# Six stages of a half share one block with named waits, and the last gate projection moves behind the attention

## What is computed

```python
h = _rmsnorm(x, norm_mix_w)
z, xbc, dt_raw, q, kv_c, kv_s, kv_w, nsa_g, br_g = _split_proj(h @ w_in)
y_ssm = mamba(z, xbc, dt_raw)                          # 32 heads, state 128
o = g0 * compressed_attention + g1 * selected_attention + g2 * window_attention
mix = sigmoid(br_g[0]) * (y_ssm @ w_ssm_branch) + sigmoid(br_g[1]) * (o @ w_attn_branch)
x = x + mix @ w_out
x = x + peer(_rmsnorm(x))     # per token 8 heads x 16 experts out of 16384, rows of peer_u, then of peer_v
y = _rmsnorm(x)
```

## Time and profile before

| | |
|---|---|
| median of 3 runs | 2726.63 us (2724.88 to 2726.69) |
| profiled execution, its time | 2727.99 us |
| its span in the trace | 2726.0 us |
| PE, DVE, POOL busy, share of the span | 74%, 54%, 54% |
| mean granted TensorE clock | 0.865 of full speed |

### The profile page before, as it was taken

How to read it: one execution, slowest core, us unless ns; L and a number is a source line. 1 busy time by engine, 2 the same in 40 slices (tenths; PEclk the granted TensorE clock), 3 DMA queues, 4 the chain that set the end, 5 groups by cost and what they waited for, 6 DMA issues and landing times. The chain is left out here.

```text
span 2726.0 us, 31394 instructions
## 1 busy us (share of the span) xinstructions
PE 2013.4 (74%) x10926; PEld 1272.5 (47%) x10926; DVE 1463.7 (54%) x3522; ACT 663.9 (24%) x1977; POOL 1472.5 (54%) x1487
## 2 busy tenths in 40 slices
PE   8999989988877989989989935754177776554054
PEld 6778865666655657644454622332154442111010
DVE  4421023247999965557621769778776764016800
ACT  5441026224545210025611122310021110000000
POOL 1110000016566865647644777777767777557775
PEclk9999989989987999989989967767589997877577
DMA  5424454446886999979889889999999999999998
GB/s 182 169 78 140 141 182 158 163 151 226 293 325 201 400 377 369 374 285 371 317 348 397 291 286 391 412 392 326 382 353 411 411 410 394 403 386 409 352 406 311
DMA packets 209781, 843.32 MB, mean 309 GB/s; under 512 B 25753, under 2 KB 32729, under 8 KB 190105
## 3 DMA queue, kind: packets, MB, share of 16 engines
q0 software_dynamic: 170912, 644.95, 62.3%
q1 hardware_dynamic: 38712, 196.36, 19.3%
HBM read 821.80 MB, written 23.54 MB: 310 GB/s over the span
## 5 line engine op out<-in xcount | busy, mean ns | idle before, releaser
L3658 POOL DMA_INDIRECT e_ring<-in_peer_u,e_idx x523 | 613.2, 1173 | 301.9 <-DVE e_dot L3822 139.0
L3822 DVE CUSTOM_DVE_ANT_0 e_ring<-e_ring,e_h 128x1024 f32<-128x1024 f32 x523 | 632.7, 1245 | 73.0 <-DMA e_ring<-in_peer_u,e_idx 25.8
L3658 POOL DMA_INDIRECT e_ring<-in_peer_v,e_idxT x487 | 506.0, 1039 | 261.6 <-issue 133.7
L3725 PE MATMUL ps<-e_ring,e_wz 128*32 128x512 f32 x1948 | 323.2, 712 | 269.4 <-DMA e_ring<-in_peer_v,e_idxT 147.4
L3725 PEld LDWEIGHTS ps<-e_ring,e_wz 128*32 128x32 f32 x1948 | 67.3, 121 | 427.3 <-issue 423.4
L371 PE MATMUL ps<-hT_ahead,wb 128*128 128x320 f32 x384 | 114.4, 454 | 0.0
L371 PEld LDWEIGHTS ps<-hT_ahead,wb 128*128 128x128 f32 x384 | 75.4, 201 | 31.2 <-issue 6.0
L3866 DVE TENSOR_TENSOR e_x<-e_x,ps 128x512 f32<-128x512 f32 x10 | 6.4, 683 | 145.7 <-PE ps L3725 145.7
L3725 PE MATMUL ps<-ring_pair,e_wz 128*32 128x512 f32 x152 | 69.7, 797 | 17.9 <-DMA e_ring<-in_peer_v,e_idxT 11.3
L1861 POOL CAST ra_atf<-ra_at 128x32 f32<-128x32 uint32 x8 | 1.7, 212 | 149.7 <-DVE ra_hit L1854 149.7
L1229 POOL MEMSET inda<- 128x256 f32 x1 | 0.3, 312 | 147.7 <-POOLq L4133 147.7
(11 more groups left out here) (789 smaller groups left out, 4577.3 us busy)
## 6 DMA issues: line engine op xcount, KB each, us to landing
wb<-in_weights SPq DMA_DIRECT2D x65, 1024.0 KB, 7.8
e_ring<-in_weights SPq DMA_DIRECT2D x36, 1024.0 KB, 4.9
wb<-in_late_weights SPq DMA_DIRECT2D x6, 2048.0 KB, 11.1
room<-in_late_weights SPq DMA_DIRECT2D x6, 2048.0 KB, 16.3
h<-in_weights SPq DMA_DIRECT2D x10, 1024.0 KB, 8.7
xs<-in_weights SPq DMA_DIRECT2D x9, 1024.0 KB, 7.9
e_ring<-in_peer_u,e_idx POOLq DMA_INDIRECT x523, 9.2
e_ring<-in_peer_v,e_idxT POOLq DMA_INDIRECT x487, 9.8
```

The source lines that it names most:

```text
L3658: nc.gpsimd.indirect_dma_start(out=self.room(place), out_offset=None, in_=k.peer_u if kind == "u" else k.peer_v, in_offset=off).then_inc(s ...
L3725: last = nc.tensor.matmul(k.ps[32 * b:32 * b + 32, self.SUMS + i, :], self.wz[:, at:at + 32], self.room(self.v_at[n])[:, 512 * i:512 * i + ...
L3822: v.tensor_tensor_reduce(uu, uu, self.h[:, tile % 2, :], 1.0, 0.0, ALU.mult, ALU.add, self.dot[:, tile % 2, t:t + 1]).then_inc(self.dotted, 1)
```

## The change

The six stages are opened in one block per half. The waits for a whole block are replaced by semaphores of single results; all semaphores live until the half's block closes. `stage_merge`, `stage_kv` and `stage_qk` are otherwise only indented anew. The cut of `stage_attn_prompt` that moves the last gate projection stands in full.

```diff
 stage_kv:
+    k.kv_done = dict(stored=(stored, len(jobs)))
-            act.wait_ge(stored, len(jobs) + 1)
 stage_qk:
+    k.qk_done = (stored, len(jobs))
                 if i >= 4:
                     pe.wait_ge(stored, i - 3)
+                else:
+                    pe.wait_ge(kv_stored, kv_jobs - 3 + i)
-            act.wait_ge(stored, len(jobs))
 stage_cmp_prompt:
         def _(sp):
+            sp.wait_ge(*k.kv_done["stored"])
...
-            sp.wait_ge(written, 16 * n)
+            k.kv_written = (written, 16 * n)
         def _(pe):
+            pe.wait_ge(*k.kv_done["stored"])
+            pe.wait_ge(*k.kv_done["masks"])
+            pe.wait_ge(*k.qk_done)
-            act.wait_ge(kept, HPK // 4)
 stage_attn_prompt:
         def _(pool):
+            if g.first:
+                pool.wait_ge(*k.cmp_done["turned"])
...
                 if d:
                     pe.wait_ge(exped, 2 * d)
+                else:
+                    pe.wait_ge(*k.cmp_done["stored"])
+                    pe.wait_ge(*k.cmp_done["kept"])
...
-                if i < N and i % 4 in LAST_OF:
+                if i < N - 4 and i % 4 in LAST_OF:
                     gate(i // 4, *LAST_OF[i % 4])
+                if i == N:
+                    gate(KD - 1, 0, KD)
                 if i >= 3 and i % 2 == 1:
                     value((i - 3) // 2)
...
+                if m == 4:
+                    act.wait_ge(*k.kv_written)
...
-                    if i % 4 == 3:
+                    if i % 4 == 3 and i < N - 4:
                         keep_gate(i // 4)
...
+            keep_gate(KD - 1)
             act.wait_ge(kept, KD)
             if g.first:
                 pages.copy(NB - 1)
...
+            dve.wait_ge(*k.cmp_done["kept"])
 stage_merge:
         def _(sp):
+            if not g.first:
+                sp.wait_ge(*k.attn_done["valued"])
             k.w.feed(sp)
         def _(pe):
+            pe.wait_ge(*k.attn_done["added"])
 stage_out:
             k.w.feed(sp, PIECES)
+            sp.wait_ge(*k.merge_done["projected"])
+            sp.wait_ge(*k.kv_written)
...
+                        if i == 0:
+                            pe.wait_ge(k.merge_done["merged"], KD - 3 + 2 * t + half)
 build:
-                    with ExitStack() as attn:
-                        allocate_attn(nc, k, attn, g)
-                        stage_kv(nc, k, g)
...
-                    stage_out(nc, k, g)
+                    with ExitStack() as links, nc.Block(no_gpsimd_drain=True) as block:
+                        with ExitStack() as attn:
+                            allocate_attn(nc, k, attn, g)
+                            stage_kv(nc, k, g, links, block)
...
+                        stage_out(nc, k, g, links, block)
```

More of the change, by code:

```diff
@@ L1141, in gate_home @@
     return k.hit[:].rearrange("p c i j -> p (c i j)")[:, 2 * P * (m - 6):2 * P * (m - 6) + 2 * P]
[L1144 to L1200, removed]
@@ L1203, in stage_kv @@
[L1203 to L1275, removed]
-            act.wait_ge(stored, len(jobs))
[L1277 to L1282, removed]
-                act.wait_ge(stored, len(jobs) + 1)
-        ex.close()
-        k.w.leave()
@@ L1344, in stage_cmp_prompt, with stage_merge, _ @@
-def stage_cmp_prompt(nc, k, g):
+def stage_merge(nc, k, g, links, block):
+    sem = lambda n: links.enter_context(nc.semaphore(f"ba{g.name}_{n}"))
+    NP = g.np
+    projected, sigmoids, merged, own_s = (sem(n) for n in ("projected", "sigmoids", "merged", "own"))
+    ex = k.ex
+    ex.plan(KD, k.share["ba"])
+    k.merge_done = dict(projected=(projected, KD), merged=merged)
+    k.w.enter(KD // 2, lambda i: (projected, 2 * i + 2))
+    @block.sync
+    def _(sp):
+        if not g.first:
+            sp.wait_ge(*k.attn_done["valued"])
+        k.w.feed(sp)
+    @block.gpsimd
+    def _(pool):
+        for m in range(KD):
+            ex.pool(m)
+    @block.tensor
+    def _(pe):
+        pe.wait_ge(*k.attn_done["added"])
+        for m in range(KD):
+            ex.pe(m)
+            pe.wait_ge(*k.w.here(m // 2))
+            if m >= 4:
+                pe.wait_ge(merged, m - 3)
+            w = k.w.view(m // 2, 2 * P)[:, :, P * (m % 2):P * (m % 2) + P]
+            for f in range(HPK):
+                last = nc.tensor.matmul(k.ps[:, m % 4, 0:NP], w[:, f, :], k.oT[:, f, :], start=(f == 0),
+                                        stop=(f == HPK - 1))
+            last.then_inc(projected, 1)
+    @block.scalar
+    def _(act):
+        for m in range(KD):
+            last = nc.scalar.activation(gate_home(k, m), gate_home(k, m), ACT.Sigmoid)
+            if g.sample:
+                last = nc.scalar.activation(k.sigs[:, 1, m, :], k.sigs[:, 1, m, :], ACT.Sigmoid)
+            last.then_inc(sigmoids, 1)
+        for m in range(KD):
+            ex.act(m)
+    @block.vector
+    def _(dve):
+        v = nc.vector
+        own = Link(dve, own_s)
+        for m in range(KD):
+            ex.dve(m)
+            dve.wait_ge(sigmoids, m + 1)
+            dve.wait_ge(projected, m + 1)
+            own(v.tensor_tensor(gate_home(k, m), gate_home(k, m), k.ps[:, m % 4, 0:NP], ALU.mult))
+            v.tensor_tensor(k.mT[:, m, :], k.mT[:, m, :], gate_home(k, m), ALU.add).then_inc(merged, 1)
+        dve.wait_ge(merged, KD)
+    ex.close()
+    k.w.leave()
@@ new lines, in stage_qk, with _ @@
+def stage_qk(nc, k, g, links, block):
+    sem = lambda n: links.enter_context(nc.semaphore(f"q{g.name}_{n}"))
+    N, NP = g.n, g.np
+    projected, stored = sem("projected"), sem("stored")
+    mine = slice(g.c0, g.c0 + NP)
+    jobs = [(k.qT[:, j, :], k.qTs[:, j, :], SCALE) for j in range(HPK)]
+    jobs += [(k.ksT[:, mine], k.ksTs[:], 1.0), (k.kwT[:, mine], k.kwTs[:], 1.0)]
+    ex = k.ex
+    ex.plan(len(jobs), k.share["qk"])
+    k.qk_done = (stored, len(jobs))
+    kv_stored, kv_jobs = k.kv_done["stored"]
+    k.w.enter(len(jobs) // 2, lambda i: (projected, 2 * i + 2))
+    @block.sync
+    def _(sp):
+        k.w.feed(sp)
+    @block.gpsimd
+    def _(pool):
+        for i in range(len(jobs)):
+            ex.pool(i)
+    @block.vector
+    def _(dve):
+        for i in range(len(jobs)):
+            ex.dve(i)
+    @block.tensor
+    def _(pe):
+        for i in range(len(jobs)):
+            ex.pe(i)
+            pe.wait_ge(*k.w.here(i // 2))
+            w = k.w.view(i // 2, 2 * P)[:, :, P * (i % 2):P * (i % 2) + P]
+            if i >= 4:
+                pe.wait_ge(stored, i - 3)
+            else:
+                pe.wait_ge(kv_stored, kv_jobs - 3 + i)
+            for f in range(KD):
+                last = nc.tensor.matmul(k.ps[:, i % 4, 0:N], w[:, f, :],
+                                        k.hT[:, f, 0:N], start=(f == 0), stop=(f == KD - 1))
+            last.then_inc(projected, 1)
+    @block.scalar
+    def _(act):
+        for i, (dst, dst_s, scale) in enumerate(jobs):
+            ex.act(i)
+            act.wait_ge(projected, i + 1)
+            last = nc.scalar.activation(dst, k.ps[:, i % 4, 0:NP], ACT.Copy, scale=scale)
+            if g.sample:
+                last = nc.scalar.activation(dst_s, k.ps[:, i % 4, NP:N], ACT.Copy, scale=scale)
+            last.then_inc(stored, 1)
+    ex.close()
+    k.w.leave()
```

155 lines of the change are left out of this document (93 added, 62 removed).

## The result

The changed kernel took 2695.73 us (median of 7 runs), the kernel before beside it 2724.88 us; the ratio over the runs is 0.9926, 95% interval 0.9899 to 0.9954. The forecast's ratio was 2715.2 / 2726.6 = 0.9958, outside that. Faster by 0.7%, and by more than forecast. In a second comparison (first experiment) the ratio was 0.995 [0.9929, 0.997], an interval that holds the forecast's ratio too.

What follows compares the result with a forecast made beforehand. PE was taken to bound both halves, transfers the stretch after. Half a 5.7 us, half b 4.2 and the merge's clock 1.5 sum to 11.4 us, taking the median from 2726.6 to 2715.2 us; range 2711 to 2719.

Steps and rivals of the forecast that it cites:

- Gaps: PE's idle time at the block ends between stages shrinks or goes; in half a 1.7, 0.4, 0.4 and 1.6 us.
- the dip at 332.3: Clock of 0.50 until 339.1 us in half a, behind keys and values; expected to stay, nothing counted.
- rival B: Clock dips behind keys and values go too, in both halves: 4.3 us more, 2710.9 us; chance 0.16.
- Gap and dip: Before and at half a's merge: block-end gap and moved projection 1.6 us net, clock dip gone 1.5 us.
- moved projection: Last gate projection put behind the attention loop; net gain with the gap 1.6 us in half a, 0.9 in half b.
- what the loop gives back: Attention's last steps shorten without the gate's pieces: 2.2 us in half a, some 1.7 in half b.
- the start of the sample stages 11 us earlier: Sign expected in the profile after: the stages behind half b begin 11 us sooner.
- the stretch behind it as long as before: Sign expected in the profile after: the time from the sample stages' start to the end stays unchanged.
- each stage there issues a fixed share of the order of gathers: Behind half b: the same work is left whenever a stage begins, so an earlier half moves all that follows equally.
- rival E: Slower: the stretch from 1588.7 us loses transfer rate; 2% gives 2738 us; chance 0.05.
- C: Half b's gain doesn't reach the end because transfers bind; 7.2 us remain, 2719.4 us; chance 0.14.
- D: Moved projection wholly in the open (-0.6 and -1 us), merge's clock not recovered: 5.8 us saved, 2720.8; chance 0.07.

Runs made afterwards that it cites:

- first experiment: The changed kernel, no edit, run again against the kernel before: ratio 0.995 [0.9929, 0.997].
- the gate alone: Kernel before with only the last gate projection moved behind the attention loop, blocks as before: 1.0027 [1.001, 1.0044].
- The kernel with waited dots: Kernel before with a DVE wait behind each of its own dots in the last stretch: 0.9998 [0.9982, 1.0013].
- five before: The kernel before's two profiles and three of kernels that edit only its end; six stages took 268.4 us in half a, 395.2 in half b.
- gelu first: Changed kernel with ACT's first expert gelu put ahead of the merge's eight sigmoids: ratio to the kernel before 0.9939 [0.9919, 0.9959].
- half b alone: Shared block in half b only, half a with its own blocks, gate projection moved in both, against the kernel before: 0.9994 [0.9975, 1.0013].
- the waits alone: The change with the gate projection back in the loop, against the kernel before: 0.9932 [0.9907, 0.9956].
- a second profile: Named waits, projection in the loop, plus DVE's wait behind each dot of the last stretch, against the kernel before: 0.9928 [0.9903, 0.9954].

## Why the prediction was right or wrong

**Gaps: right.** Forecast in half a were 1.7, 0.4, 0.4 and 1.6 us for keys and values, queries, compressed attention and merge. Keys and values gave 1.9; idle time fell from 0.93 to 0.56, from 1.13 to 0.77 and from 1.57 to nothing. In half b keys and values gave 1.0 us (43.7 to 42.7) where 0.9 was forecast. The merge's weights made nobody wait.

**Clock, the step that failed.** The prediction said of the dip at 332.3: "It began as the block ended, not after a gap, so I leave it in", and so counted nothing for it. Seven profiles have the block end there in half a and six of them the dip: queries of 37.4 to 38.3 us, where the one without has 35.8. Seven have no block end, and one of them has the dip (37.0 against 35.3). In half b the queries take 54.2 to 54.3 us instead of 52.6 in four of seven with the block end, in none of seven without. That is rival B, priced at 2.5 + 1.8 us: it came with 6 in 7 and 4 in 7, about 3 us in all. The Trainium skill (TensorE: Matmul & The Clock Gate, "What's actually happening") makes activity what releases the throttle, and the simple reading of it, which I had ranked second, gave the better number. The traces don't bear out the cause that this reading names, the standstill. In five of the six the clock fell between 0.28 us before and 0.11 us after the last gate matmul ended, so PE had hardly stood, or not at all. In the sixth, the gate alone, it fell 2.7 us after that end, with the queries running. The kernel with waited dots shows it best; there PE stood from 330.64 to 332.33 us:

```profile
327.00:330.36 3.36, 3.36 (x33) 3.36 (x31) 0.00 (x0) 0.59 (x2) 0.00 (x0) 1.00 0.70 212
330.36:330.64 0.28, 0.28 (x2) 0.12 (x1) 0.00 (x0) 0.00 (x0) 0.00 (x0) 0.50 1.10 468
```

What does differ is the length: the clock stayed at 0.50 for 6.8 us in these five, and for 3.4 us in the gate alone and in the one profile without a standstill. So the removed block end goes with fewer dips, one in seven instead of six; what sets them off stays open.

The merge of half a is the second part of it. Gap and dip were priced from the first profile, 1.6 + 1.5 = 3.1 us. There the merge took 30.8 us, with the clock at 0.50 for 3.4 us; in four others of the five it took 32.3 to 32.5 us, with 6.8 us at 0.50, so that both were worth 4.4 on the mean. Half a as a whole gave 268.4 - 257.2 = 11.2 us where 5.7 + 1.5 = 7.2 were forecast: keys and values 1.9 (forecast 1.7), queries 2.9 (0.4), compressed attention 0.5 (0.4), last steps 1.5 (1.6), merge 4.4 (3.1).

**The moved projection: its sum held in half a and failed in half b.** Forecast were +1.6 us in half a and +0.9 in half b, net of the gap. Last steps of half a: 20.3 on the mean of five before, 18.8 after; the loop gave 1.7 of the expected 2.2. Last steps of half b: 40.3 on the mean of five before, 40.6 and 40.7 after, a loss of 0.3 and not a gain of 0.9. There the term that failed is what the loop gives back: steps 28 to 31 took 16.1 us before and 15.8 after, 0.3 us where 1.7 was counted. But there are four orders, not two (last steps and merge together, means of the profiles in each, two to six of them; gelu first is left out):

```
                       half a   half b
block end, in loop     52.2     85.7
block end, moved       53.6     87.2
wait, moved            46.5     84.6
wait, in loop          45.4     76.5
```

Moving costs 1.4 and 1.5 us behind a block end, 1.1 in half a behind a wait, and 8.1 in half b behind a wait. The reason is in the rows above. Behind the wait and with the projection in the loop, ACT begins its sigmoids 10.6 us after the last scores (1356.82 - 1346.20); behind the moved projection it is 16.7 (1368.30 - 1351.60). I compared the new order with the old one, in which the block end held ACT. So I never priced what the wait gives by itself, 85.7 - 76.5 = 9.2 us, nor that the projection takes 8.1 of it back; putting the gelu first recovers 6.0 of these (36.6 + 42.0 = 78.6). Half b in all: 395.2 - 391.7 = 3.5 us against 4.2 forecast, near by two errors that cancel, waits worth more and the projection costing more.

**Sum.** By stages 11.2 + 3.5 = 14.7 us, 0.9946, in agreement with 0.995; the first comparison's 0.9926 reaches to 0.9954. The forecast was 11.4 us, 0.9958, which the second comparison holds as well, so the times don't tell 14.7 from 11.4; the stages of half a do. At the first matmul of the sample stages 10.5 us are left, on the mean of two profiles against five, since the stretch between the halves takes 505.6 to 511.1 us in one profile or another, whatever the edit. So the sign "the start of the sample stages 11 us earlier" came, and "the stretch behind it as long as before" didn't: 11.1 of its 14.0 us are the last stretch. The rest of the first 29 us between medians is, as far as the runs tell, spread, above all of the kernel before: its first three runs lay within 2 us, but over all comparisons its runs lie between 2702 and 2737 us. My range took in the bounds of the edits and nothing for that. Its margins came from one profile and three runs, and the step "each stage there issues a fixed share of the order of gathers", from which I took it that the stretch keeps its length, hid a stretch that is 198 or 211 us by itself. That is rival E's place, with a sign that the edits don't set.

**Rivals C and D.** C, that half b's gain doesn't reach the end: half b alone, 0.9994, can't refute it. The traces speak against it up to the last stretch. From the first matmul of the sample stages to gather 1000 it takes 894.3 us on the mean of five profiles before, 894.2 in the two of the change and 892.1 in the two of the waits alone, though these begin 10.5 and 23.4 us earlier: what is gained ahead isn't lost there. D: half a's loop gave back and its merge's clock recovered, so it fell there; in half b its direction was right, with -0.3 us where D had -1.

**Beyond the change.** Keeping the waits and leaving the projection in the loop is the best version by stages (254.5 and 382.5 us, or 257.8 and 386.2 us in a second profile; half b is clear of the change's 391.6 both times). By time it stands at 0.9932 and 0.9928 in two comparisons, the change at 0.9926 and 0.995: the runs don't separate them.

## What to carry to other kernels

Price a moved piece of work against the order that the rest of the edit makes, not against the old one: a wait removed for ACT was worth 9.2 us in half b, and 1.1 us once new work stood ahead of the same engine. When block ends go, count the clock stretches around them in several profiles and not in one. Before trusting a range of a few us, find the stretch of the kernel that differs between executions of the same program; it may be as wide as the effect.

## What the runs showed of the hardware

POOL's issue of an indirect gather took 0.94 us beside an idle DVE, up to 1.98 us beside 128x1024 multiply-and-sum operations of DVE on two SBUF operands that start every 1.15 us, and 0.96 us when a wait makes them start every 1.27 us: none of the 65 issues beside them took over 1.2 us then. Not each issue is slow at 1.15 us: where DVE was late, issues of 0.94 us stand between those of 1.98. The Trainium skill (SBUF — State Buffer, "SBUF: two separate sides") says that DVE and GpSimd share a pair of ports by an exclusive lock, which a DVE operation with two SBUF inputs can take, though only against a GpSimd operation that reads SBUF. The trace agrees in that a tenth of a us between two operations decides whether the issue passes at once; that it is this lock, and not another resource of the two engines, no run here shows.

TensorE's granted clock fell to 0.50 in six of seven executions in which PE stood still between the 48-column matmuls and the queries of half a (1.7 us in the first), and in one of seven in which it didn't stand there. In five of the six the fall came within 0.3 us of the end of the last 48-column matmul, in one of them while they still ran (the windows from 327.00 us above). At the gap of 1.57 us between merge and output projection it didn't fall: 32 matmuls took 13.97 us, in the same profile.
